# A gated linear attention stage: where tile 1's attention products and turns go, and output rows done tile by tile

## What is computed

```python
def gla_mixer(h, w_in, w_alpha, b_alpha, norm_g, w_out):
    proj = h @ w_in
    q, k, v, r, z = jnp.split(proj, [GLA_QK, 2 * GLA_QK, 2 * GLA_QK + D_MODEL,
                                     2 * GLA_QK + 2 * D_MODEL], axis=-1)
    log_alpha = jax.nn.log_sigmoid((z @ w_alpha + b_alpha).astype(jnp.float32)) / GLA_TAU
    ...
    o = gla_chunk_scan(to_chunks(q * (GLA_DK ** -0.5), GLA_DK), to_chunks(k, GLA_DK),
                       to_chunks(v, GLA_DV), to_chunks(log_alpha, GLA_DK))
    o = o.transpose(1, 0, 3, 2, 4).reshape(bsz, s, GLA_HEADS, GLA_DV)
    o = rmsnorm(o, norm_g).reshape(bsz, s, D_MODEL).astype(h.dtype)
    return (o * jax.nn.silu(r)) @ w_out
```

## Time and profile before

| | us |
|---|---|
| median of 3 runs | 2749.5 |
| lowest, highest | 2748.26, 2751.53 |
| the profiled execution | 2747.3 |
| its span, first to last instruction | 2745.5 |
| TensorE busy (share of the span) | 2659.9 (97%) |
| GpSimd | 1973.2 (72%) |
| ScalarE | 1387.4 (51%) |
| VectorE | 1028.6 (37%) |
| mean granted TensorE clock | 0.986 |

### The profile page before, as it was taken

One profiled execution on the slowest core, in us unless ns is written; L12 is line 12 of the kernel. 1 busy time (PEld: TensorE's weight loads), 2 busy tenths in 40 slices (PEclk: granted clock), 3 DMA queues, 4 the chain that ended last, 5 costly groups with the idle time before them and its releaser, 6 DMA issues.

```text
span 2745.5 us, 35973 instructions
## 1 busy us (share of the span) xinstructions
PE 2659.9 (97%) x15016; PEld 2276.4 (83%) x15016; DVE 1028.6 (37%) x1695; ACT 1387.4 (51%) x1667; POOL 1973.2 (72%) x432
## 2 busy tenths in 40 slices
PE   7899988999999999999999999999999999999998
PEld 4789976799888778888888888888878888877887
DVE  6968867443212453121124311212441131245312
ACT  3754554555544455445455444544544454455543
POOL 3677764588787748878876688787648878774885
PEclk8999989999999999999999999999999999999999
DMA  8769842365555435546553455555425555543552
GB/s 325 281 231 360 322 161 108 139 223 185 201 186 182 177 115 198 185 169 215 193 185 144 153 199 186 198 188 180 154 106 205 195 192 192 184 170 122 188 196 108
DMA packets 80390, 521.78 MB, mean 190 GB/s; under 512 B 8908, under 2 KB 9292, under 8 KB 24420
## 3 DMA queue, kind: packets, MB, share of 16 engines
q1 hardware_dynamic: 73316, 494.30, 50.0%
q10 hardware_dynamic: 6912, 25.17, 2.3%
HBM read 518.38 MB, written 1.05 MB: 189 GB/s over the span
## 4 chain that ended last, share of the span: by engine, by line
PE 89%; DVE 7%; ACT 2%; DMA 1%; issue 0%; POOL 0%; SPq 0%; DVEq 0%; ACTq 0%
PE acc L555 17%; PE acc L594 16%; PE mb L532 11%; PE cb L532 11%; PE cb L507 10%; PE cb L534 6%; PE mb L534 6%; PE mb L647 2%; PE acc L859 1%; DVE hT L1859 1%; PE acc L507 1%; PE cb L820 1%; PE cb L647 1%; PE mb L844 1%; PE acc L482 1%; ACT whi L1171 1%
## 5 line engine op out<-in xcount | busy, mean ns | idle before, releaser
L2496 POOL TENSOR_TENSOR wlo<-raw,whi 128x2048 fp32r<-128x2048 f32 x428 | 1972.9, 4621 | 748.9 <-ACT whi L1171 675.3
L1171 ACT ACTIVATE whi<-raw 128x2048 fp32r<-128x2048 f32 x428 | 818.3, 1915 | 588.0 <-PE cb L532 250.0
L555 PE MATMUL acc<-whi,ARR 128*128 128x512 f32 x1312 | 367.9, 392 | 4.6 <-DVE ARR L1859 4.6
L532 PE MATMUL cb<-hT,whi 128*128 128x512 f32 x1280 | 335.4, 393 | 0.0
L532 PE MATMUL mb<-hT,whi 128*128 128x512 f32 x1280 | 334.1, 393 | 0.1
L555 PEld LDWEIGHTS acc<-whi,ARR 128*128 128x128 f32 x1312 | 246.5, 189 | 58.1 <-issue 7.7
L507 PE MATMUL cb<-hT,whi 128*128 128x256 f32 x1536 | 280.2, 284 | 0.0
L594 PE MATMUL acc<-whi,hT 128*128 128x512 f32 (+2 forms) x928 | 260.3, 389 | 7.1 <-DVE hT L1859 5.7
L532 PEld LDWEIGHTS mb<-hT,whi 128*128 128x128 f32 x1280 | 230.2, 189 | 43.8 <-issue 2.9
L532 PEld LDWEIGHTS cb<-hT,whi 128*128 128x128 f32 x1280 | 229.6, 189 | 40.5
L1928 DVE TENSOR_TENSOR cb<-cb,AR 128x512 f32<-128x512 f32 x80 | 56.0, 700 | 552.2 <-ACT AR L1179 552.1
(11 more groups left out here) (323 smaller groups left out, 3414.3 us busy)
## 6 DMA issues: line engine op xcount, KB each, us to landing
raw<-in_w SPq DMA_DIRECT2D x436, 1024.0 KB, 4.8
AR<-in_a SPq DMA_DIRECT2D x32, 512.0 KB, 5.6
AR<-in_a ACTq DMA_DIRECT2D x32, 512.0 KB, 6.2
z<-in_a ACTq DMA_DIRECT2D x16, 512.0 KB, 6.7
gb<-in_lng SPq DMA_DIRECT2D x12, 512.0 KB, 5.7
gb<-in_lnb SPq DMA_DIRECT2D x12, 512.0 KB, 6.6
gb<-in_normg SPq DMA_DIRECT2D x8, 512.0 KB, 7.1
x<-in_x SPq DMA_DIRECT2D x1, 1024.0 KB, 8.5
```

What stands on the lines that cost most here:

```text
L532: ins = pe.matmul(to[j], wh[:, w], hT[:, k, :], start=k == 0, stop=k == 7)
L555: ins = pe.matmul(acc[:, 2 * t + c, 0:c1 - c0], xs[y], a[:, kk * width + c0:kk * width + c1], start=first and kk == 0 and m == 0, stop=las ...
L1171: ac.activation(whi[i % NH][:, :], raw[u % NR][:, :], ACT.Copy).then_inc(*up(s_hi, ("hi", i)))
L2496: po.tensor_tensor(wlo[i % NH][:, :], raw[(i + NADA) % NR][:, :], whi[i % NH][:, :].bitcast(F32), ALU.subtract).then_inc(*up(s_lo, ("lo", i)))
```

## The change

Tile 1's attention products go to acc 2 and 3 instead of cb. Tile 0's turns go to the two cb banks, tile 1's to acc 2 and 3. The output rows are one `rows_units` call over all four units: all 48 products of tile 0, then all 48 of tile 1. A generator `beside_rows` issues tile 1's turns and the six vector sums between tile 0's products, one piece after every fourth product from the sixteenth on. The next stage's tile 0 is turned when eight products of tile 1 are left. `ready` waits for the tile's own turned halves alone. VectorE takes all six sums at unit 60's place. `sums` loses the two entries and `taken` gets one.

ScalarE no longer calls `out_units` here. Its conversions of units 64, 65 and 66 stand together at the boundary, behind tile 0's norm and ahead of tile 0's turned copies and of tile 1's squares. At that boundary VectorE does the low halves of tile 0's turns ahead of tile 1's multiply by gt.

```diff
--- before.py
+++ after.py
@@ -171,7 +171,7 @@
 
                 sums.setdefault(h + 2, []).append((v, half))
                 taken.setdefault(h + 3, []).append((v, half))
-    sums[FIRST[3] - 4], sums[FIRST[3] - 3] = [(8, 0), (8, 1), (9, 0)], [(9, 1), (10, 0), (10, 1)]
+    taken[FIRST[3] - 4] = [(v, half) for v in (8, 9, 10) for half in range(2)]
     for h in sums:
         if not FIRST[1] <= h < FIRST[2]:
             taken[h] = sums[h]
@@ -781,7 +781,7 @@
                 scores(0)
                 for t in range(2):
                     for hp in range(2):
-                        to = claim(bank("cb"), ("go", t, hp))
+                        to = claim(("acc", 2 + hp) if t else bank("cb"), ("go", t, hp))
                         q.wait_ge(*on("attn"))
                         q.wait_ge(*on("gv", 1))
                         for j in range(2):
@@ -791,21 +791,34 @@
                                 ins = pe.matmul(to[:, j * 256:j * 256 + 256], lhs, g_v3[:, kt, hd * 256:hd * 256 + 256],
                                                 start=kt == 0, stop=kt == t)
                         ins.then_inc(*up(s_mm, ("full", ("go", t, hp))))
-                for t in range(2):
+
+                def turn_result(t, half):
+                    to = claim(("acc", 2 + half) if t else bank("cb"), ("gy", t, half))
+                    q.wait_ge(*on("gz", t))
+                    for j in range(4):
+                        i = 4 * half + j
+                        ins = pe.transpose(to[:, j * 128:j * 128 + 128], z[:, t, i * 128:i * 128 + 128], ident)
+                    ins.then_inc(*up(s_mm, ("full", ("gy", t, half))))
+
+                def beside_rows():
+
                     for half in range(2):
-                        to = claim(bank("mb"), ("gy", t, half))
-                        q.wait_ge(*on("gz", t))
-                        for j in range(4):
-                            i = 4 * half + j
-                            ins = pe.transpose(to[:, j * 128:j * 128 + 128], z[:, t, i * 128:i * 128 + 128], ident)
-                        ins.then_inc(*up(s_mm, ("full", ("gy", t, half))))
+                        turn_result(1, half)
+                        yield
+                    for v in (8, 9, 10):
+                        for half in range(2):
+                            vector_sum(v, half)
+                            yield
 
                 def ready(t, k):
-                    for tt in range(2):
-                        q.wait_ge(*on("gyh", tt, k // 4))
-                        q.wait_ge(*on("gyl", tt, k // 4))
-
-                out_units(n, lh, ll, ready)
+                    q.wait_ge(*on("gyh", t, k // 4))
+                    q.wait_ge(*on("gyl", t, k // 4))
+
+                turn_result(0, 0)
+                turn_result(0, 1)
+                beside = beside_rows()
+                rows_units([(2 * j, 2 * j + 1) for j in range(4)], lh, ll, ready, ("sum", n), first=True, last=True,
+                           beside=beside, after=12, every=4, at_half=beside, early=[(8, lambda: turn(n + 1, 0))])
 
             def scores_of(name, parts, kind, ready):
 
@@ -1221,7 +1234,7 @@
                 if b < 5:
                     gated(b, 0)
                     norm(b, 0)
-                    if b % 2:
+                    if b == 1:
                         gated(b, 1)
                         turned(b, 0)
                         highs(h - 2 + NH)
@@ -1482,7 +1495,6 @@
                         key = ("gy", t, half)
                         q.wait_ge(*on("full", key))
                         copy(hTh[:, 4 * half:4 * half + 4, t * 128:t * 128 + 128], c3(view(key), 4), ("gyh", t, half))
-                out_units(n)
 
             def exps(name, i):
                 t, h0 = order[name][i]
@@ -1880,11 +1892,11 @@
                 if b < 5:
                     gated(b, 0)
                     norm(b, 0)
-                    if b % 2 == 0:
+                    if b > 1:
 
                         turned(b, 0)
                     gated(b, 1)
-                    if b % 2:
+                    if b == 1:
                         turned(b, 0)
                     norm(b, 1)
                     return
@@ -2198,7 +2210,7 @@
                         q.wait_ge(*on("gyh", t, half))
                         low_of(hTl[:, 4 * half:4 * half + 4, sl], c3(view(key), 4), hTh[:, 4 * half:4 * half + 4, sl],
                                ("gyl", t, half), ("free", key))
-                out_units(n)
+                unit(FIRST[n + 1] - 4)
 
             def biased(name, i):
```

## The result

The changed kernel takes 2734.2 us, against 2748.9 before: a ratio of 0.9945 (95% interval 0.9934 to 0.9957), 14.7 us less, and its time is 0.4 below the range. These are medians of four executions each. With the later series, 14 executions of the change have a mean of 2734.8 and 89 of the kernel before one of 2748.3: 13.5 us less (standard error of the difference 0.5). The forecast was 11.8 us less.

A forecast was written before the change was run, and what follows sets the result against it. TensorE, busy for 97% of the span, bounds the kernel, so only its idle stretches offer a gain. Terms -11.0, -1.6, +1.2, 0, +1.0 and -1.4 came to -11.8 us: 2749.5 to 2737.7, range 2734.6 to 2742.6.

The forecast's parts named there:

- Tile 1's products and the rows' start, -11.0: GLA's end: with tile 1's products in the gate's banks, output rows start at about 471.7 instead of 482.73, -11.0 us.
- The clock, -1.6: Output rows' start: TensorE keeps 2.4 GHz, so the first 24 products cost 5.46 instead of 7.09 us, -1.6.
- Work between the rows, +1.2, 0 and +1.0: Output rows: tile 1's turns inside the pass +1.2 us, the six vector sums 0, the next tile 0's turns +1.0.
- T: End of tile 0's pass of output rows, predicted 17.3 us after their start, at 489.0.
- The boundary, -1.4: Boundary to conv1: from the rows' end to tile 1's turns 7.6 us instead of 9.0, -1.4.
- The rest unchanged: Behind tile 1's turns at conv1: everything stands as before, so the gain of 11.8 us carries whole to the end.
- The base: Time of the kernel before, 2749.5 us, from which the forecast took the 11.8 us gain.
- the clock's fall: Rival: TensorE falls to 1.2 GHz in the rows, 2739.3, or also at conv1's head, up to 2742.1; chance 0.35.
- The port's effect: Rival at tile 1's norm: GpSimd's unit 65 conversion blocks VectorE's multiply up to 4.6 us, up to 2741.9; chance 0.07.
- More than forecast: Rival: tile 0's low halves or the sums overlap better, another 1 to 2 us, 2736; chance 0.05.
- the banks do not help: Rival at GLA's end: tile 1's products still wait, keeping about 4 us and the fallen clock, 2743.3; chance 0.04.

## Why the prediction was off

The mechanism, its places and the direction were right. A size was off: the gain came out at 13.5 us over all executions (14.7 in the first series) instead of 11.8. By the steps, with the first pair of profiles:

- **Tile 1's products and the rows' start, -11.0.** This is the step that failed. The kernel before starts its rows 20.69 us after L791 in the profile that I read, and 21.78 in the third; the changed one after 9.27. So this term is -11.4 in one case and -12.5 in the other. 0.4 of it are links between ScalarE and VectorE that I had put too long. The other 1.1 are the clock: "sixteen end near 467.6 instead of 473.1" took one execution's 5.41 us for the kernel's, and where the clock falls differs between executions. Of the four profiles with this wait, two show 5.41 us and two 6.49 and 6.48, so the mean price lies some 0.5 us above mine, as far as four profiles tell.
- **The clock, -1.6.** This was right for the rows: 24 products took 7.09 us before. Now they take 6.46 with tile 1's turns between them, and some 5.5 in the run that has these turns in a block. It isn't all that the clock is worth. With tile 1's products and the turns at the lower clock, which stand in the term above, it is 4.5 to 4.8 us, and 5.8 against the third profile of the kernel before, by TensorE's busy time (46.0 instead of 40.2).
- **Work between the rows, +1.2, 0 and +1.0.** Tile 0's pass ended 17.36 us after the first row, against 17.3, and the rows ended at T + 11.6 against T + 11.9. With the clock's part the two passes were to take 0.6 us more than before and took 0.3 more, since tile 1's turns cost 0.9 us and not 1.2. That the sums cost the same alone as in threes held: in a block they save 0.4 us at most.
- **The boundary, -1.4.** Measured -1.6 (7.4 us from the rows' end to the turns, against 9.0). TensorE waited 1.41 us for unit 65, against my 1.3; the multiply lost 0.60, against 0.4, and ScalarE was done with its conversions at T + 10.8 and not 11.2.
- **The rest unchanged.** This was right, 2225.0 us in both.
- **The base.** I took the gain off 2749.5, the median of three executions. The mean of 89 is 2748.3, so the forecast of the time stood 1.2 us too high before any term.

The measured 2734.2 is 3.5 us below the forecast of 2737.7. Of that, 1.2 are the base, 0.8 the terms in the first pair of profiles (12.6 instead of 11.8), some 0.5 the clock's earlier fall in part of the executions, and 0.7 the four executions of the first series, whose median is below the mean of all 14. The remaining 0.3 is within the standard error. By the mean of 14, 2734.8, the time would lie just inside the range, so the miss of the range is partly chance; that the gain was put too low isn't. Whether the clock at conv1's head, which fell in two of the five profiles with the old boundary, adds to the price of the kernel before in some executions stays open: in its own three profiles it did not fall there.

The range allowed 3.1 us below the forecast for all this, and nearly all of what can go wrong I had put on the slow side.

Of the rivals, the clock's fall was not seen in any of the three profiles of the change, neither in the rows nor at conv1's head. The port's effect is real: it cost 0.6 us as it stands, 4.1 when provoked. "More than forecast" came nearest to the time, but not by its reasons, since the low halves were worth 0.5 us and the place of the sums 0.4 at most. And "the banks do not help" was priced too low at 2743.3, for it left out the lower clock under tile 1's products: with the old banks the kernel takes 2745.3.

## What to carry to other kernels

When a wait is removed on a 97% busy TensorE, add to its length what the clock loses in it and behind it (here 4.8 us beside 7.8 of waits), and take that from several profiles, since where the clock falls differs from one execution to the next. Take the base from more than three executions, too. When a pass over tiles is reordered, ask when it releases its buffers and which engine's queue then stands behind them: here two conversions left in their old place beside the new order cost 11.5 us, nearly the whole gain. Where the time of two kernels is close, cut their traces at the same events and compare the pieces; it shows at once what belongs to the change.

## What the runs showed of the hardware

- A multiply-add on two SBUF operands beside a GpSimd conversion took 5.35 us instead of 1.28, a multiply 3.75 instead of 1.23. With one operand in PSUM the same kinds of operation kept 1.28 and 1.23 us beside a conversion.
- The clock's fall depends on work and not on results: 32 unread products, put into waits of 1.4 to 3.7 us, kept it at 2.4 GHz there, and the kernel became 3.2 us faster by doing more.
- The same wait can leave the clock up in one profile and not in another. At conv1's head 1.6 and 1.07 us of idleness were followed by 1.00 in the three profiles of the kernel before and by 0.50 in two others.
- The same code ahead of the change ended anywhere from 459.2 to 464.4 us in thirteen profiles.
